# An expert stage in fp32: quarter-row gathers turned on VectorE in place of TensorE, and the gated product's transposes in two groups

## The chip, the core and the metric
The kernel runs on one core of a Trainium2 chip, as one program. The metric is device time in microseconds of one execution. The runs of the kernel before lie within 0.3% of each other. All data are float32.

## What is computed
The reference is one layer of a language model over 2048 prompt tokens and 128 sample tokens: a mixer (depthwise convolution and spatial gating), attention into 256 memory tokens, and a mixture of experts with a final norm. Only the last part matters here:

```python
# hier_moe: top-1 of 4 groups, then top-2 of 8 experts in it; D = 1024, 32 experts of width 512
def expert_block(args):                      # one block of rows that go to one expert
    xb, e = args
    return (jax.nn.silu(xb @ w_eg[e]) * (xb @ w_eu[e])) @ w_ed[e]
...
x = x + hier_moe(rms_norm(x, g_ffn), ...)    # gate weight times each expert's row, added to x
y = rms_norm(x, g_final)
```

## The kernel before, in words
**Stages.** The mixer and attention into memory come first. The last stage (one block of code from line 1289 on) has two parts: 17 tiles of 128 tokens go through scores, values, the router and the placing of each token's two assignments into a table in DRAM; then the expert steps run. The two parts overlap a little: the first expert tile is fetched while the last tiles are still in attention.

**An expert step** (`work(t)` on every engine, tiles t = 0 to 41) takes 64 rows of an expert of the lower 16 and 64 rows of one of the upper 16. The rows are those of `h3_d`, the normalised tokens. TensorE's helper `both` (lines 2206 and 2207) issues two matmuls of 64 stationary columns each, one per expert, into the upper and lower half of a PSUM tile; each is two records in the trace, since the data are fp32. In a step TensorE does, in this order:
- the gate product (8 k-chunks, 512 columns, into `psg`), then the up product in two halves of 256 columns (8 k-chunks each, into `ups[0]`, a part of `r_pss`, and `ups[1]`, a part of `r_psk`);
- `turn_h(t, 0)`: two 128x128 transposes of the first half of the gated product `hb`; `turn_x(t + 1)`: eight transposes of the next tile's gathered rows `xg` into `pst`; `turn_h(t, 1)`: the other two of `hb`;
- the down product (4 k-chunks, two halves of 512 columns, into `psx`), 16 pairs of matmul records.

**VectorE** in a step: `tokens(t + 2)` (one cast of 128 row numbers, line 1957), `rows(t)` (lines 1985 and 1986), `hidden(t)` (two products of silu and up, line 1974), `hT_out` (line 1979), `xT_out(t + 1)` (line 1962, chunks 4 to 7), `add_x(t)` (line 1993: the weighted result added to x, two halves), `scale(t)` (the final norm). **ScalarE**: silu (1770), `hT_out` (1775, the first two chunks in one copy), `xT_out` (1780, chunks 0 to 3), the squares of the final norm (1800). **GpSimd** issues the small transfers: `gather_x(t)` (1608, rows of x), `gather(t + 2)` (1600, rows of h3, 4 KB each), `fetch(t + 3)` and `fetch_again(t + 1)` (1584, two transfers of 64 table rows each), `scatter_x(t)` (1614), a power (1621), `scatter_out(t)` (1627). `gather_x(t)` waits until the scatter of t - 1 has landed.

**SyncE** loads the weights with `load_part` (line 1286), 2 MB each for gate, up and down of an expert, as soon as the slot's last reader of that part is done. The upper experts have one slot, the lower ones two that alternate.

**Order of the work.** Each engine's program is written out by hand, with one counting semaphore per kind of event (`T["h_done"]`, `T["xT_done"]`, ...). `need(eng, sem, n)` is a wait that is left out where n is 0 or less. An engine runs its own program in order, so whatever stands behind a wait waits too.

**The start of the expert steps** has a chain without overlap: the last rank gives the last table scatter, then `fetch(1)`, `tokens(1)` on VectorE, `gather(1)` on GpSimd, `turn_x(1)` on TensorE, the two `xT_out` copies, and the gate product of tile 1. VectorE's program there is `tokens(1)`, `add_x(0)`, a copy of the load list, `tokens(2)`, `xT_out(1)`; GpSimd's is `fetch(1)`, `gather(1)`, `fetch(2)`, `fetch_again(1)`, `scatter_x(0)`.

`turn_split` (line 220) already exists, for the attention tiles. It transposes 32x32 blocks on VectorE, of a tile whose DMA has put the quarter-rows of 32 tokens into each group of 32 partitions. It gives chunk k of the contraction the columns j of which j mod 8 is k.

## Time and profile before
| what | value |
|---|---|
| median of 3 runs | 2452.66 us (2451.31 to 2457.74) |
| the profiled execution: its own time | 2455.3 us |
| its span, first to last instruction | 2453.6 us |
| TensorE busy | 2385.9 us, 97% |
| VectorE busy | 1015.2 us, 41% |
| GpSimd busy | 560.1 us, 23% |
| ScalarE busy | 448.8 us, 18% |
| DMA | 427.31 MB, 174 GB/s over the span |

The span is 1.7 us shorter than the execution's own time, and that execution was 2.6 us above the median. A busy TensorE is one that has a matmul in flight; back-to-back matmuls overlap, so the distance from start to start, not the duration, says what one costs. The expert steps run from 1524.9 us to the end.

### The profile page before, as it was taken

Reading aid. Unit: us, or ns where it says so; the run is one execution under the profiler, and the core shown is the slowest. Engines: PE = TensorE matmul, PEld = TensorE weight load, DVE = VectorE, ACT = ScalarE, POOL = GpSimd, SP = SyncE. Lnnn points to the kernel's source line nnn. Section 1 sums busy time; section 2 is a strip of 40 time slices with the busy share of each in tenths; the row PEclk is TensorE's granted clock in tenths of the full one; section 3 lists DMA queues with packets and bytes.
Section 4 is the critical chain, followed back from the end, with each engine's and each line's share of the span. In section 5 each row is a group of like instructions: output and inputs, shape, how many; then the busy total and the mean of one; then the engine's idle time right before and its main releaser. Section 6 shows DMA issues by size and latency. Waiting matters only on the chain.

```text
span 2453.6 us, 33018 instructions
## 1 busy us (share of the span) xinstructions
PE 2385.9 (97%) x10639; PEld 1161.2 (47%) x10640; DVE 1015.2 (41%) x2549; ACT 448.8 (18%) x1012; POOL 560.1 (23%) x711
## 2 busy tenths in 40 slices
PE   8999999999999997999999998999999999999998
PEld 4444444444444474444444443444444444444443
DVE  1585665666678112255555543222222222222222
ACT  2222212212211122111111111111111111111111
POOL 1122232132133000011111113232323322323231
PEclk9999999999999999999999999999999999999999
DMA  6202111111132436464444327967497749797994
GB/s 238 108 30 67 39 41 58 39 53 47 40 126 106 149 127 223 148 191 124 122 130 127 117 86 271 340 220 270 169 366 264 261 165 368 262 353 270 350 353 149
DMA packets 186898, 427.31 MB, mean 174 GB/s; under 512 B 27874, under 2 KB 51962, under 8 KB 186666
## 3 DMA queue, kind: packets, MB, share of 16 engines
q1 hardware_dynamic: 155810, 351.41, 42.0%
q0 software_dynamic: 30656, 74.14, 8.3%
q8 instruction: 53, 0.87, 0.1%
q10 hardware_dynamic: 336, 0.54, 0.1%
q14 instruction: 43, 0.35, 0.0%
HBM read 351.89 MB, written 88.52 MB: 179 GB/s over the span
## 4 chain that ended last, share of the span: by engine, by line
PE 57%; DMA 1%; DVE 1%; issue 0%; POOL 0%; ACT 0%; POOLq 0%; SPq 0%; DVEq 0%; ACTq 0%
PE r_pss L2206 17%; PE r_psx L2206 12%; PE r_psx L2165 10%; PE r_pss L2145 9%; PE r_psk L2206 6%; PE r_pst L2195 2%; PE r_psr L2177 1%; PE r_psr L2215 1%; PE r_pss L2215 0%; PE r_pss L2207 0%; DMA table_scratch<-r_val,r_slot 0%; PE r_pss L2251 0%; DMA r_x1n<-h_scratch,e_token 0%; PE r_psx L2207 0%; PE r_psk L2207 0%
## 5 line engine op out<-in xcount | busy, mean ns | idle before, releaser
L790 PE MATMUL a_psz<-W 128*128 128x512 f32 x1088 | 480.0, 594 | 0.1
L2206 PE MATMUL r_pss<-W,r_h2T 128*64 x1312 | 432.3, 488 | 3.3 <-issue 3.3
L2207 PE MATMUL r_pss<-W,r_h2T 128*64 128x256 f32 (+1 forms) x1312 | 432.3, 488 | 0.0
L628 DVE SCALAR_TENSOR_TENSOR yacc<-aext,pcol,yacc 128x256 f32<-128x256 f32 x928 | 370.8, 477 | 0.0
L790 PEld LDWEIGHTS a_psz<-W 128*128 128x128 f32 x1088 | 203.2, 191 | 235.5 <-issue 235.0
L2206 PEld LDWEIGHTS r_pss<-W,r_h2T 128*64 128x64 f32 x1312 | 180.1, 137 | 257.3 <-issue 215.8
L2207 PE MATMUL r_psx<-W,r_x1r 128*64 128x512 f32 x656 | 290.3, 595 | 0.0
L2206 PE MATMUL r_psx<-W,r_x1r 128*64 x656 | 290.3, 595 | 0.0
L2165 PE MATMUL r_psx<-W 128*128 128x512 f32 x544 | 237.6, 594 | 1.2 <-ACT W L1724 1.2
L2145 PE MATMUL r_pss<-W,r_h2T 128*128 128x512 f32 x512 | 225.4, 598 | 2.3 <-PEq L123 2.3
L2207 PEld LDWEIGHTS r_pss<-W,r_h2T 128*64 128x64 f32 x1312 | 180.1, 137 | 0.0
L492 POOL TENSOR_TENSOR W<-W 128x512 f32<-128x512 f32 x34 | 115.6, 3408 | 267.0 <-ACT W L605 267.0
L2206 PEld LDWEIGHTS r_psx<-W,r_x1r 128*64 128x64 f32 x656 | 86.5, 137 | 170.7 <-issue 170.7
L2165 PEld LDWEIGHTS r_psx<-W 128*128 128x128 f32 x544 | 102.1, 190 | 123.8 <-issue 123.8
L2145 PEld LDWEIGHTS r_pss<-W,r_h2T 128*128 128x128 f32 x512 | 96.6, 191 | 118.4 <-issue 118.4
L1993 DVE SCALAR_TENSOR_TENSOR r_x<-r_psx,e_spair,r_x 128x512 f32<-128x512 f32 x84 | 63.0, 751 | 213.6 <-PE r_psx L2207 213.6
L2207 PE MATMUL r_psk<-W,r_h2T 128*64 128x256 f32 x656 | 148.3, 379 | 0.0
L2206 PE MATMUL r_psk<-W,r_h2T 128*64 x656 | 148.3, 379 | 0.0
L957 PE MATMUL a_psz<-W,a_maT 128*128 128x512 f32 x272 | 122.3, 592 | 0.0
L957 PE MATMUL a_psz<-W 128*128 128x512 f32 x272 | 122.3, 592 | 0.0
L1614 POOL DMA_INDIRECT x_scratch<-r_x,e_stoken x41 | 42.7, 1042 | 324.7 <-DVE r_x L1993 304.8
L1974 DVE TENSOR_TENSOR r_x1r<-r_pss,r_x1r 128x256 f32<-128x256 f32 x43 | 18.1, 423 | 229.5 <-PE r_pss L2207 229.5
(358 smaller groups left out, 2618.8 us busy)
## 6 DMA issues: line engine op xcount, KB each, us to landing
W<-in_w_expert_gate SPq DMA_DIRECT2D x32, 2048.0 KB, 12.1
W<-in_w_expert_up SPq DMA_DIRECT2D x32, 2048.0 KB, 11.0
W<-in_w_expert_down SPq DMA_DIRECT2D x32, 2048.0 KB, 10.3
W<-in_x_prompt SPq DMA_DIRECT2D x32, 512.0 KB, 4.2
x_scratch<-W SPq DMA_DIRECT2D x18, 512.0 KB, 3.0
r_x1r<-x_scratch SPq DMA_DIRECT2D x17, 512.0 KB, 4.4
x_scratch<-r_x SPq DMA_DIRECT2D x17, 512.0 KB, 5.2
h_scratch<-r_h SPq DMA_DIRECT2D x17, 512.0 KB, 2.6
```

Source lines behind the costliest of these rows:

```text
L492: pool.tensor_tensor(x, mixed[:, 512 * n:512 * n + 512], x, ALU.add).then_inc(S["x1_half"], 1)
L628: ins = dve.scalar_tensor_tensor(out=out, in0=src, scalar=w, in1=yacc[:, i, :], op0=ALU.mult, op1=ALU.add)
L790: last = pe.matmul(psz[bank][:], hT[t.par][:, k, :], w_in[bank][:, k, :], start=(k == 0), stop=(k == KD - 1))
L957: last = pe.matmul(psz[n][:], (maT[:, k, :] if k < CG else mbl[t.par][:, k - CG, :]), w_out[:, k, 512 * n:512 * n + 512], start=(k == 0), ...
L1614: pool.indirect_dma_start(out=x2_d.rearrange("t p d -> (t p) d"), out_offset=bass.IndirectOffsetOnAxis(ap=stoken[t.par][:], axis=0), in_=y ...
L1993: dve.scalar_tensor_tensor(out=yb[t.par][:, c], in0=psx[:, c], scalar=spair[t.par][:, 1:2], in1=yb[t.par][:, c], op0=ALU.mult, op1=ALU.add ...
L2145: last = pe.matmul(pss[:, 2 * n:2 * n + 2, :].rearrange("p h n -> p (h n)"), h2T[i % 2][:, k, :], A[:, k, 512 * n:512 * n + 512], start=(k ...
L2165: last = pe.matmul(psx[:, 512 * n:512 * n + 512], (pT if i else qT)[:, c, :], (B if i else w_xo)[:, c, 512 * n:512 * n + 512], start=(c == ...
L2177: last = pe.matmul(psr[:, 0:NG + NE], h3T[:, k, :], wr[:, k, :], start=(k == 0), stop=(k == KD - 1))
L2195: last = pe.transpose(pst[:, k, :], xg[t.par][:, P * k:P * k + P], ident[:])
L2206: pe.matmul(out[0:HALF, :], xt[:, 0:HALF], W[:, bass.ds(base + at, n)], start=start, stop=stop)
L2207: return pe.matmul(out[HALF:P, :], xt[:, HALF:P], W[:, at:at + n], start=start, stop=stop)
```

## The change
The x rows are gathered as quarter-rows and turned on VectorE:
- `token` gets four columns. `tokens(t)` makes 16 small VectorE operations of 32 partitions each, out of one quarter of the row numbers into another quarter of the partitions, 4 times the number plus the quarter.
- `gather(t)` issues four indirect transfers of 128 quarter-rows (1 KB each) in place of one of 128 rows.
- `turn_x` and the semaphore `x_turned` go; both `xT_out` copies (ScalarE and VectorE) become one `turn_split` on VectorE, which waits for the gathers themselves. `xT_done` counts once a tile.
- `load_part` reads gate and up weights as `a (p k) n` in place of `a (k p) n`, so that the contraction is cut the same way; each partition then reads 8 adjoining rows.

The transposes of the gated product stand elsewhere: `turn_h(t, 0)` between chunks 3 and 4 of the second up half, `turn_h(t, 1)` after the first two of the down product's eight calls of `both`. The down product takes chunk 0, chunk 1, then chunks 2 and 3; ScalarE copies chunks 0 and 1 one by one.

```diff
-                          I[name][0][bass.ds(e, 1), :, :].rearrange("a (k p) n -> p (a k) n", p=P)).then_inc(here, 16)
+                          I[name][0][bass.ds(e, 1), :, :].rearrange("a (k p) n -> p (a k) n" if n == 2 else "a (p k) n -> p (a k) n", p=P)).then_inc(here, 16)
...
-            token = [sb(f"e_token{i}", [P, 1], I32) for i in range(2)]
+            token = [sb(f"e_token{i}", [P, QUADS], I32) for i in range(2)]
...
                     def gather(t):
                         pool.wait_ge(T["token_done"], t.v + 1)
-                        need(pool, T["x_turned"], 2 * (t.v - 1))
+                        need(pool, T["xT_done"], t.v - 1)
                         settle(pool)
-                        pool.indirect_dma_start(out=xg[t.par][:], out_offset=None,
-                                                in_=h3_d[0:P * (EARLY + 2), :] if isinstance(t.v, int) and t.v == 0 else h3_d,
-                                                in_offset=bass.IndirectOffsetOnAxis(ap=token[t.par][:], axis=0)).then_inc(x_here[t.par], 16)
+                        h3_rows = h3_d[0:P * (EARLY + 2), :] if isinstance(t.v, int) and t.v == 0 else h3_d
+                        for b in range(QUADS):
+                            c = D // QUADS
+                            pool.indirect_dma_start(out=xg[t.par][:, c * b:c * b + c], out_offset=None,
+                                                    in_=h3_rows.rearrange("t (q c) -> (t q) c", q=QUADS),
+                                                    in_offset=bass.IndirectOffsetOnAxis(ap=token[t.par][:, b:b + 1], axis=0)).then_inc(x_here[t.par], 16)
...
-                        act.activation(hT[:, 0:2, :], psh[:, 0:2, :], ACT.Copy).then_inc(T["hT_lo"], 1)
-
-                    def xT_out(t):
-                        act.wait_ge(T["x_turned"], 2 * t.v + 1)
-                        need(act, T["up_done"], t.v)
-                        act.activation(xT[t.par][:, 0:4, :], pst[:, 0:4, :], ACT.Copy).then_inc(T["xT_done"], 1)
+                        for k in range(2):
+                            act.activation(hT[:, k, :], psh[:, k, :], ACT.Copy).then_inc(T["hT_lo"], 1)
...
                     def tokens(t):
                         dve.wait_ge(pair_here[t.par], 32 * (t.half + 1))
-                        need(dve, x_here[t.par], 16 * t.half)
-                        dve.tensor_copy(token[t.par][:], pair[t.par][:, 0:1]).then_inc(T["token_done"], 1)
+                        need(dve, x_here[t.par], 16 * QUADS * t.half)
+                        for b in range(QUADS):
+                            for q in range(QUADS):
+                                last = dve.tensor_scalar(token[t.par][QUAD * q:QUAD * q + QUAD, b:b + 1], pair[t.par][QUAD * b:QUAD * b + QUAD, 0:1],
+                                                         float(QUADS), float(q), ALU.mult, ALU.add)
+                        last.then_inc(T["token_done"], 1)
 
                     def xT_out(t):
-                        dve.wait_ge(T["x_turned"], 2 * t.v + 2)
+                        dve.wait_ge(x_here[t.par], 16 * QUADS * (t.half + 1))
                         need(dve, T["up_done"], t.v)
-                        dve.tensor_copy(xT[t.par][:, 4:8, :], pst[:, 4:8, :]).then_inc(T["xT_done"], 1)
+                        turn_split(dve, xT[t.par][:], xg[t.par][:]).then_inc(T["xT_done"], 1)
...
-                        pe.wait_ge(T["xT_done"], 2 * t.v + 2)
+                        pe.wait_ge(T["xT_done"], t.v + 1)
...
                             for k in range(KD):
+                                if m and k == KD // 2:
+                                    turn_h(t, 0)
                                 last = both(ups[m], xT[t.par][:, k, :], base, 4096 + 512 * k + 256 * m, k == 0, k == KD - 1, 256)
                             last.then_inc(T["up_done" if m else "up_half"], 1)
-                        turn_h(t, 0)
-                        if j < LAST - 1:
-                            turn_x(t.at(1), (0, 1, 2, 3))
-                            turn_x(t.at(1), (4, 5, 6, 7))
-                        turn_h(t, 1)
                         pe.wait_ge(down_here, wanted)
                         need(pe, F["added"], 2 * t.v)
-                        for m in range(2):
-                            pe.wait_ge(T["hT_hi" if m else "hT_lo"], t.v + 1)
+                        for k in range(2):
+                            pe.wait_ge(T["hT_lo"], 2 * t.v + k + 1)
                             for n in range(2):
-                                for k in (2 * m, 2 * m + 1):
-                                    last = both(psx[:, 512 * n:512 * n + 512], hT[:, k, :], base, 8192 + 1024 * k + 512 * n, k == 0, k == KE - 1)
-                                if m:
-                                    last.then_inc(T["down_done" if n else "y_half"], 1)
+                                both(psx[:, 512 * n:512 * n + 512], hT[:, k, :], base, 8192 + 1024 * k + 512 * n, k == 0, False)
+                            if k == 0:
+                                turn_h(t, 1)
+                        pe.wait_ge(T["hT_hi"], t.v + 1)
+                        for n in range(2):
+                            for k in (2, 3):
+                                last = both(psx[:, 512 * n:512 * n + 512], hT[:, k, :], base, 8192 + 1024 * k + 512 * n, False, k == KE - 1)
+                            last.then_inc(T["down_done" if n else "y_half"], 1)
```

The same edits are made for tiles 0 and 1, whose code stands outside the steps: `turn_x(0)` between the two halves of the last attention tile's scores goes, `xT_early` on VectorE becomes one `turn_split`, `turn_x(1)` ahead of the steps goes, and `gate_early` waits for `xT_done`.

## Rows read from the trace of the kernel before

**Rows 1.** The page: the chain that ended last, by line, in shares of the span.
```profile
PE r_pss L2206 17%; PE r_psx L2206 12%; PE r_psx L2165 10%; PE r_pss L2145 9%; PE r_psk L2206 6%; PE r_pst L2195 2%; PE r_psr L2177 1%; PE r_psr L2215 1%; PE r_pss L2215 0%; PE r_pss L2207 0%; DMA table_scratch<-r_val,r_slot 0%; PE r_pss L2251 0%; DMA r_x1n<-h_scratch,e_token 0%; PE r_psx L2207 0%; PE r_psk L2207 0%
```

**Rows 2.** Groups by line and shape from 1400 us on: busy us, mean ns | idle before, releaser.
```profile
L2195 PE MATMUL r_pst<-ident,r_x1n 128*128 128x128 f32 x336 | 44.5, 276 | 7.1 <-DMA r_x1n<-h_scratch,e_token 7.1
```

**Rows 3.** TensorE's timeline around one step's transposes: start us, us, engine, line, operation.
```profile
2007.96 0.38 PE L2206 MATMUL r_psk<-W,r_h2T 128*64 x1
...
2008.17 0.38 PE L2206 MATMUL r_psk<-W,r_h2T 128*64 x1
...
2008.49 0.44 PE L2215 MATMUL r_psr<-ident,r_x1r 128*128 128x128 f32 x2
...
2009.95 0.64 PE L2206 MATMUL r_psx<-W,r_x1r 128*64 x1
...
2010.43 0.59 PE L2206 MATMUL r_psx<-W,r_x1r 128*64 x1
...
2030.74 0.44 PE L2215 MATMUL r_psr<-ident,r_x1r 128*128 128x128 f32 x2
```

**Rows 4.** TensorE's timeline around the first tile's x transposes, in the attention stage.
```profile
1441.52 1.04 PE L2195 MATMUL r_pst<-ident,r_x1n 128*128 128x128 f32 x8
1442.39 1.45 PE L2145 MATMUL r_pss<-W,r_h2T 128*128 128x512 f32 x3
```

**Rows 5.** VectorE's timeline in one step.
```profile
1999.38 0.14 DVE L1985 CAST e_stoken<-e_spair 128x1 int32<-128x1 f32 x1
1999.44 0.14 DVE L1986 CAST f_oidx<-e_spair 128x1 int32<-128x1 f32 x1
2005.22 0.42 DVE L1974 TENSOR_TENSOR r_x1r<-r_pss,r_x1r 128x256 f32<-128x256 f32 x1 [5.63 <-PE r_pss L2207]
2008.61 0.43 DVE L1974 TENSOR_TENSOR r_x1r<-r_psk,r_x1r 128x256 f32<-128x256 f32 x1 [2.96 <-PE r_psk L2207]
```

**Rows 6.** VectorE's timeline early in the kernel: line 663 in a loop over partition halves.
```profile
27.42 1.14 DVE L663 TENSOR_SCALAR W<-W 64x576 f32<-64x576 int32 x2
```

**Rows 7.** Timelines of VectorE, GpSimd and TensorE where the expert stage starts; one granted clock.
```profile
1446.95 2.03 DVE L222 STREAM_TRANSPOSE r_h3T<-r_h3s 128x1024 f32<-128x1024 f32 x1 [4.92 <-DMA r_h3s<-h_scratch]
...
1515.82 0.15 DVE L1957 CAST e_token<-e_pair 128x1 int32<-128x1 f32 x1 [6.62 <-DMA e_pair<-table_scratch]
...
1517.14 1.03 POOL L1600 DMA_INDIRECT r_x1n<-h_scratch,e_token  x1 [5.14 <-issue]
...
1519.40 0.52 POOL L1584 DMA_DIRECT2D e_pair<-table_scratch  x1 [0.63 <-issue]
...
1522.48 0.15 DVE L1957 CAST e_token<-e_pair 128x1 int32<-128x1 f32 x1 [5.01 <-DMA e_pair<-table_scratch]
...
1524.90 1.11 PE L2206 MATMUL r_pss<-W,r_h2T 128*64 x1 [0.98 <-issue]
...
1519.60:1529.70 10.10, 6.77 (x20) 3.06 (x22) 2.62 (x7) 1.93 (x5) 5.11 (x9) 0.50 0.43 148
```

**Rows 8.** GpSimd's timeline in one step.
```profile
2018.67 1.04 POOL L1614 DMA_INDIRECT x_scratch<-r_x,e_stoken  x1 [10.13 <-DVE r_x L1993]
...
2028.78 1.00 POOL L1608 DMA_INDIRECT r_x<-x_scratch,e_stoken  x1 [5.10 <-DMA x_scratch<-r_x,e_stoken]
2030.08 0.96 POOL L1600 DMA_INDIRECT r_x1n<-h_scratch,e_token  x1 [0.30 <-issue]
...
2034.48 0.52 POOL L1584 DMA_DIRECT2D e_spair<-table_scratch  x1 [0.73 <-issue]
```

**Rows 9.** Issue to landing of line 1600 (x gathers), then of line 1584 (pair fetches).
```profile
DMA to landing us min/median/max: 4.4/7.7/10.2
...
DMA to landing us min/median/max: 1.7/5.5/8.6
```

**Rows 10.** Busy time by stretch: PE, PEld, DVE, ACT, POOL, clock, DMA share, GB/s.
```profile
2000.00:2100.00 100.00, 100.00 (x650) 48.24 (x648) 22.01 (x48) 13.60 (x31) 31.49 (x41) 1.00 0.98 353
...
5.00:10.00 5.00, 1.89 (x9) 1.75 (x9) 0.73 (x3) 2.16 (x3) 3.68 (x7) 1.00 1.05 394
```

More of the change, by code:

```diff
@@ L1409, in build @@
             e_names = ("counted listed turned placed sorted link steps_known slots_known loads_known count_known "
-                     "token_done stoken_done x_turned xT_done gate_done up_half up_done down_done y_half silu_done h_done h_turned "
+                     "token_done stoken_done xT_done gate_done up_half up_done down_done y_half silu_done h_done h_turned "
                      "hT_lo hT_hi").split()
@@ L1687, in work @@
                             for i in range(2):
-                                pool.wait_ge(x_here[i], 16 * (pairs + LAST // 2))
+                                pool.wait_ge(x_here[i], 16 * QUADS * (pairs + LAST // 2))
                                 settle(pool)
@@ L1787, in _ @@
                     for m in range(2):
-                        act.activation(hT[:, 2 * m:2 * m + 2, :], psh[:, 2 * m:2 * m + 2, :], ACT.Copy).then_inc(T["hT_hi" if m else "hT_lo"], 1)
-                    act.wait_ge(S["s_psum"], NT - 1)
-                    xT_out(fixed(1))
+                        act.activation(hT[:, 2 * m:2 * m + 2, :], psh[:, 2 * m:2 * m + 2, :], ACT.Copy).then_inc(T["hT_hi" if m else "hT_lo"], 1 if m else 2)
                     def squares(t):
@@ L1808, in work @@
                         hT_out(t)
-                        if j < LAST - 1:
-                            xT_out(t.at(1))
-                        else:
-                            act.wait_ge(T["xT_done"], 4 * (pairs + 2))
-                            settle(act)
+                        if j == LAST - 1:
                             act.wait_ge(F["sample_here"], 16)
@@ L2014, in xT_early @@
                         dve.wait_ge(S["s_psum"], NT - 2)
-                        dve.wait_ge(T["x_turned"], 2)
-                        for m in range(2):
-                            dve.tensor_copy(xT[0][:, 4 * m:4 * m + 4, :], pst[:, 4 * m:4 * m + 4, :]).then_inc(T["xT_done"], 1)
+                        dve.wait_ge(x_here[0], 16 * QUADS)
+                        turn_split(dve, xT[0][:], xg[0][:]).then_inc(T["xT_done"], 1)
                     for s in range(NT):
@@ L2134, in turn_p @@
                         pe.wait_ge(S["prob_done"], i)
-                        pe.wait_ge(T["xT_done"], 2)
+                        pe.wait_ge(S["squares1"], NT - 1)
                         for k in range(KD):
@@ L2189, in ranks @@
                         pe.matmul(psk[:, 0:NE], ones[:], total[:], start=False, stop=True).then_inc(S["rank_psum"], 1)
-                    def turn_x(t, ks):
-                        if ks[0] == 0:
-                            pe.wait_ge(x_here[t.par], 16 * (t.half + 1))
-                            need(pe, T["xT_done"], 2 * t.v)
-                        for k in ks:
-                            last = pe.transpose(pst[:, k, :], xg[t.par][:, P * k:P * k + P], ident[:])
-                        if ks[-1] in (3, 7):
-                            last.then_inc(T["x_turned"], 1)
                     def weights(t):
@@ L2211, in turn_h @@
                         if m == 0:
-                            need(pe, T["hT_lo"], t.v)
+                            need(pe, T["hT_lo"], 2 * t.v)
                             need(pe, T["hT_hi"], t.v)
@@ L2231, in work @@
                             for k in range(KD):
+                                if m and k == KD // 2:
+                                    turn_h(t, 0)
                                 last = both(ups[m], xT[t.par][:, k, :], base, 4096 + 512 * k + 256 * m, k == 0, k == KD - 1, 256)
                             last.then_inc(T["up_done" if m else "up_half"], 1)
-                        turn_h(t, 0)
-                        if j < LAST - 1:
-                            turn_x(t.at(1), (0, 1, 2, 3))
-                            turn_x(t.at(1), (4, 5, 6, 7))
-                        turn_h(t, 1)
                         pe.wait_ge(down_here, wanted)
                         need(pe, F["added"], 2 * t.v)
-                        for m in range(2):
-                            pe.wait_ge(T["hT_hi" if m else "hT_lo"], t.v + 1)
+                        for k in range(2):
+                            pe.wait_ge(T["hT_lo"], 2 * t.v + k + 1)
                             for n in range(2):
-                                for k in (2 * m, 2 * m + 1):
-                                    last = both(psx[:, 512 * n:512 * n + 512], hT[:, k, :], base, 8192 + 1024 * k + 512 * n, k == 0, k == KE - 1)
-                                if m:
-                                    last.then_inc(T["down_done" if n else "y_half"], 1)
+                                both(psx[:, 512 * n:512 * n + 512], hT[:, k, :], base, 8192 + 1024 * k + 512 * n, k == 0, False)
[6 more added lines that the diff above has]
+                            last.then_inc(T["down_done" if n else "y_half"], 1)
                     def product(out, k, at, stop):
@@ L2257, in gate_early @@
                             pe.wait_ge(S["exp_done"], NT - 1)
+                            pe.wait_ge(T["xT_done"], 1)
                         for k in ks:
```

6 lines of the change are left out of this document (removed).

## The prediction, made before the changed kernel was run

> **What bounds the kernel now.** I read the chain that ended last first, since it says which engine's work the end hangs on. Of the expert stage it holds the gate, up and down products, and also 2% of `r_pst L2195`, the transposes of the gathered rows: about 49 us that multiply nothing [rows 1]. Next, TensorE's waits: over all 336 of these transposes (42 tiles of 8) it stood still before them for 7.1 us in total, and that in one place, the stage's start [rows 2]. So in the steps TensorE waits for nobody, and a step lasts as long as TensorE takes to issue it. Two steps' transposes stand at 2008.49 and 2030.74, which makes 22.25 us a step [rows 3]. An instruction taken off TensorE shows in the time at once; one given to another engine is free as long as that engine keeps up. The start of the stage is the other way round: there TensorE waits for a chain through VectorE, GpSimd and a DMA.
>
> **TensorE's part of a step.** Pairs of 256-column matmuls start 0.215 us apart (2007.96, 2008.17), so 512 columns take 0.43. From the last up pair at 2008.17 to the second down pair at 2010.43 are 2.26 us; less 0.215 and 0.43, the twelve transposes between cost 1.615 [rows 3]. A transpose by itself: eight from 1441.52 to 1442.39, 0.109 each, 12 make 1.31 [rows 4]. The other 0.31 is what it costs to go into the group and out of it: the first transpose comes 0.32 after the last pair, not 0.215, and the second down pair 0.48 after the first, not 0.43.
>
> After the change four transposes are left, 4 x 0.109 = 0.44, in two groups. What a group costs beyond its own time no row shows for the new places. Bounds: 0.31, as the group behind 256-column pairs has it [rows 3], and nothing, as the group between 512-column matmuls of the attention stage, from which the next matmul starts right behind the eighth transpose [rows 4]. The group in the second up half is of the first kind, and I take 0.31; the one in the down product stands between 512-column pairs, but of 64 stationary columns, and the wait for the down weights stays behind the up pairs, so I take half, 0.15. New: 0.44 + 0.31 + 0.15 = 0.90, a saving of 0.72 a step (0.56 with both at 0.31, 1.18 with both at nothing). Forty steps turn a next tile (42 less tiles 0 and 1): 40 x 0.72 = **28.7 us**, bounds 22.4 and 47. The last step has no x to turn, but it has the two groups; from its own gap I put 0.3. Tile 0's eight transposes leave the attention stage, where TensorE is busy on both sides: 0.87 [rows 4].
>
> **Do the moved transposes find their data?** `turn_h(t, 0)` needs the first gated half, a product of 0.42 us from 2005.22 on, done at 2005.64 [rows 5]. The second up half's first pair is 15 x 0.215 before 2008.17, at 2004.95; eight pairs later is 2006.67: 1.0 us to spare. The second half's product starts at 2008.61 and ends at 2009.04 [rows 5]; the new `turn_h(t, 1)` comes four down pairs after the up half's end, at 2008.39 + 1.72 = 2010.1: 1.1 to spare. Its copy (0.42 to 0.43 like the products) has the 1.72 us of chunk 1 as cover. If one of them came late, TensorE would stand for the difference.
>
> **VectorE's part.** `tokens` goes from one operation to 16. Bounds for one: 0.06, as the casts at 1999.38 and 1999.44 follow each other [rows 5], and 0.18. The upper one comes from a loop that, like the new one, changes the group of partitions from one operation to the next with no wait between: two of 0.55 us take 1.14 together, so the second starts only when the first has ended, 0.03 later [rows 6]; with 0.15 for a small operation [rows 7] that is 0.18. I take 0.18, the row of the same kind: 15 x 0.18 = 2.7 more. In a step VectorE idles 5.63 us before the first gated half [rows 5], so 2.7 fit, and 2.9 are left. The 32x32 transpose of a tile takes 2.03 [rows 7]; in a step it stands after the second copy, about 1.94 + 0.6 into the down product, and ends at 4.6, before three quarters of that product (5.15), where `add_x` can begin. Cost nothing; if VectorE were late there, `scale` and the next `hidden` would be.
>
> The Trainium skill ("VectorE: DVE Perf Modes", section "Two Vector instructions with no wait between them") has this as a rule: an instruction whose output starts in another quadrant than the last one's is held until all earlier ones have finished. By that rule each of the 16 is held; the trace agrees. Were it not so, the start below would be 3.6 us cheaper.
>
> **GpSimd's part.** Three more gathers; one follows another after 1.3 us (2028.78 to 2030.08) [rows 8]: 3.9 us a step. It idles 10.13 us before this scatter, 5.10 before this `gather_x` [rows 8], so they are covered unless the loop under the slower rival closes. The 0.5 MB a tile stay the same.
>
> **The start of the stage**, where nothing covers. Before: `tokens(1)` at 1515.82, gather at 1517.14, second transfer of `fetch(2)` at 1519.40, `tokens(2)` at 1522.48, gate product at 1524.90 [rows 7]. After: the gathers begin 2.7 later, at 1519.84, and the fourth at 1523.74; the fetch, 2.26 behind the last gather as before, at 1526.0; it lands as before 3.08 later, 1529.1. `tokens(2)` stands before `xT_out(1)` on VectorE, so the transpose waits for it: 1529.1 + 16 x 0.18 + 2.03 = 1534.0, and the gate product starts at 1534.2: **9.3 us later** (5.6 with operations of 0.06). The rows themselves have landed by then (4.4 to 10.2 after the issue [rows 9]; above 8.2 they would be last). TensorE's clock stands at 0.50 from 1519.6 to 1529.7 [rows 7], half speed, after it had been idle; it will again fall in the longer idle time and rise after a stretch of work. Before, 5 us of gate product ran at half speed; I put no difference, within 1 us either way.
>
> **The rest at nothing:** ScalarE loses a copy and gets one more; the one transpose for tile 0 on VectorE takes some 0.8 us more than two copies, ahead of a softmax whose result TensorE takes up much later; the weights' new order moves the same bytes in longer runs.
>
> **Sum:** -28.7 - 0.3 - 0.9 + 9.3 = -20.6. Against the profiled execution, 2455.3 (its span and 1.7 around it), that is 2434.7; that execution was 2.6 above the median of 2452.66, so I predict **2432 us**, 0.84% less. Its own range: at best 0.87 a step (one group at 0.31, one at nothing), 5.6 for the start and 1 us of the clock, 2421; at worst 0.56 a step and 10.3, 2440.
>
> **Rivals.**
> 1. *Both groups cost nothing beyond themselves.* 40 x 1.18 = 47 saved, in all -39: 2414. For it: the attention stage's group [rows 4]. Against: the group behind 256-column pairs cost 0.31 [rows 3]. Chance 0.07.
> 2. *The DMA engines become the bound of the steps with loads.* From 2000 to 2100 their share is 0.98 at 353 GB/s [rows 10]; a step shorter by 0.72 with the same bytes asks for 365. If these steps (27 loads of 6 MB lie in 40 steps) keep 22.25 us, only 13 x 0.72 = 9.4 are saved, in all about -2: **2451**. Against: 394 GB/s have been moved at 5 to 10 us [rows 10], and longer runs should not be slower. Chance 0.11.
> 3. *GpSimd's queue becomes the loop: slower.* A scatter at 2018.67 must land before `gather_x` at 2028.78, the last fetch starts at 2034.48 [rows 8]; 3.9 more puts it at 2038.4, and a landing of 8.6 [rows 9] at 2047.0. VectorE needs the pairs before it can make the next gated half, at 2005.22 + 2 x 22.25 - 0.7 = 2049.0, and TensorE has 1.0 behind that: 3.0 us of slack. The gathers' landings show 7.7 as median and 4.4 as least [rows 9], so other traffic costs them 3.3. If that price goes by the number of descriptors, four times as many could make it 13, 10 more. It decides from 3.8 us of added latency on: 0.8 x 25 loaded steps = 20, the saving. At 4.5 more: 1.5 x 25 = 38, in all +17: **2470**. Against: the bytes are the same, and most waits of the queue have slack. Chance 0.12. 
> 4. *The change doesn't do what it says*: a moved group waits for its data and takes the saving back. The margins of 1.0 and 1.1 us speak against it; a loss of 0.3 a step gives 2444. Chance 0.05.
>
> **The numbers.** The forecast has 0.65. Within 0.3% (7.4 us, about what a measurement of this kernel can tell from no change) lies rival 2, and slower is rival 3. Faster: 0.65 + 0.07 + 0.05 = 0.77. The range 2421 to 2451 takes in the forecast's own and rivals 2 and 4, and leaves out 0.07 and 0.12.
>
> **What the profile will show.** No L2195; two groups of two transposes per step, the distance between steps 21.5 us; sixteen operations of VectorE 0.18 apart; four gathers 1.3 apart; the first gate product of the steps near 1533. I am wrong if steps lie more than 21.8 us apart with TensorE not waiting (a group costs more), if TensorE waits for `hb` copies or weights in loaded steps (rivals 4 and 2), if VectorE waits for `e_spair` (rival 3), or if the start is over 11 us later.

## The result, and the profile after

The changed kernel measured **2484.3 us** (median of 4, 2483.1 to 2486.9) beside 2452.0 for the one before: 1.0128 times as long, interval 1.011 to 1.0146. The forecast was 2432, so by this measurement it was wrong, on the other side. It is also a number that did not come back: the same kernel, unedited, in five later measurements on four chips, took 2440.8, 2437.6, 2437.8, 2440.4 and 2440.9, that is 0.9928 to 0.9946 times the kernel before (intervals within 0.9907 to 0.9967). The kernel before took 2451.0 to 2457.7 beside the 2484 and 2450.5 to 2456.3 beside the five, so whatever made 2484 left it alone. (One execution of the kernel before, beside the first edits, took 5140 us; it stands alone, is in no ratio, and nothing shows its cause.) Both have to be read: what made 2484, and what the change is worth without it.

First the profile of the 2484 execution (span 2481.4). Its page, the chain that ended last, by engine:

```profile
PE 48%; another core or an unknown queue 7%; issue 2%; DVE 1%; DMA 1%; POOL 0%; ACT 0%; POOLq 0%; SPq 0%; ACTq 0%; DVEq 0%
```

Seven per cent hang on something that the profile can't name. The chain of waits by engine, from 1534 to 2440 (who waited for whom: us, times, longest), for TensorE, then ScalarE and VectorE:

```profile
PE r_psx L2192 <- ACT r_x1r L1779: 17.0, 12, 1.7
PE r_psx L2192 <- DVE r_x1r L1975: 13.3, 19, 1.2
...
ACT r_x1r L1779 <- remote: 99.0, 13, 7.8
...
DVE r_x1r L1975 <- remote: 62.0, 19, 3.9
```

TensorE waits for the two copies of the turned gated product (L1779 on ScalarE, L1975 on VectorE), and these wait for something that the profile calls "remote", which is an update that it can match to no instruction's end, though all that they need is TensorE's own transposes. The two rows add up to 30.3 us, where the prediction had nothing. The timeline of one such step:

```profile
1654.06 0.44 PE L2201 MATMUL r_psr<-ident,r_x1r 128*128 128x128 f32 x2
1654.07 0.95 POOL L1603 DMA_INDIRECT r_x1n<-h_scratch,e_token  x1 [0.30 <-issue]
...
1655.33 0.94 POOL L1603 DMA_INDIRECT r_x1n<-h_scratch,e_token  x1 [0.30 <-issue]
...
1656.00 0.38 PE L2193 MATMUL r_psk<-W,r_h2T 128*64 128x256 f32 x1
1656.27 1.18 POOL L1584 DMA_DIRECT2D e_pair<-table_scratch  x2
1657.37 1.10 POOL L1584 DMA_DIRECT2D e_spair<-table_scratch  x2
1657.48 0.45 ACT L1779 ACTIVATE r_x1r<-r_psr 128x128 f32<-128x128 f32 x2 [7.80 <-remote]
1657.56 0.42 DVE L1970 TENSOR_TENSOR r_x1r<-r_psk,r_x1r 128x256 f32<-128x256 f32 x1 [4.61 <-PE r_psk L2193]
...
1658.00 0.64 PE L2192 MATMUL r_psx<-W,r_x1r 128*64 x1 [1.62 <-ACT r_x1r L1779]
```

The two transposes end at 1654.50 and the last up product at 1656.38. Both tell the other engines by a semaphore (`h_turned` and `up_done`), and both signals arrive close together, at 1657.4 and 1657.5: 2.9 and 1.2 us late. TensorE itself went on without a gap until it needed the copy. I call these *late updates*. Counted from the trace's semaphore events, 35 of the 81 recorded updates of `h_turned`, 27 of the 41 of `up_done` and 3 of the 41 of `up_half` came over 0.3 us after their instruction's end (the expectations below say 36 of 78 for `h_turned`: a first count over a shorter stretch, in which an update without a record passed for a late one). No recorded update of ScalarE or VectorE did, though that trace misses 19 of the 82 of `h_done`; in the trace of before none of any engine's was late. Every one of them overlaps a stretch in which GpSimd issues gathers or fetches.

Now the same kernel in after_fourth (span 2437.5). Its chain by line, which answers to [rows 1], holds no transposes of rows any more, and 2% for the gated product's:

```profile
PE r_pss L2192 16%; PE r_psx L2192 11%; PE r_psx L2160 10%; PE r_pss L2140 9%; PE r_psk L2192 6%; PE r_psr L2172 1%; PE r_psr L2201 1%; PE r_pss L2201 1%; PE r_pss L2238 0%; DMA x_scratch<-r_x,e_stoken 0%; PE r_pss L2193 0%; PE r_psx L2276 0%; PE r_psx L2193 0%; PE r_psk L2193 0%; PE r_psk L2184 0%
```

TensorE's waits over the stretch from 1534 to 2440:

```profile
PE r_pss L2192 <- issue: 2.5, 1, 2.5
PE r_psr L2201 <- DVE r_x1r L1970: 1.2, 1, 1.2
```

and the rows of one of its steps on TensorE, which answer to [rows 3]:

```profile
2041.64 0.38 PE L2192 MATMUL r_psk<-W,r_h2T 128*64 x1
...
2041.96 0.44 PE L2201 MATMUL r_psr<-ident,r_x1r 128*128 128x128 f32 x2
2042.33 0.43 PE L2192 MATMUL r_psk<-W,r_h2T 128*64 x1
...
2042.60 0.38 PE L2192 MATMUL r_psk<-W,r_h2T 128*64 x1
...
2043.89 0.38 PE L2192 MATMUL r_psk<-W,r_h2T 128*64 x1
...
2044.11 0.59 PE L2192 MATMUL r_psx<-W,r_x1r 128*64 x1
...
2045.39 0.59 PE L2192 MATMUL r_psx<-W,r_x1r 128*64 x1
...
2045.92 0.44 PE L2201 MATMUL r_pss<-ident,r_x1r 128*128 128x128 f32 x2
2046.29 0.64 PE L2192 MATMUL r_psx<-W,r_x1r 128*64 x1
...
2046.77 0.59 PE L2192 MATMUL r_psx<-W,r_x1r 128*64 x1
...
2063.64 0.44 PE L2201 MATMUL r_psr<-ident,r_x1r 128*128 128x128 f32 x2
```

From one step's first group to the next: 2063.64 - 2041.96 = 21.68, where before had 22.25. In the 2484 execution the shortest distance is 21.68 too, and most lie at 22.4 to 23.6, 22.93 on average, against 21.82 in after_fourth: (22.93 - 21.82) x 40 = 44 us, and the two spans differ by 43.9.

Where the 16.1 us between before's and after_fourth's profiled spans come from (each segment is a difference of two starts in the timelines; the routing stage's last product is that of `p_at_place`):

| segment | before | after_fourth | difference |
|---|---|---|---|
| start to the routing stage's last product | 1514.66 | 1514.51 | -0.15 |
| from there to the first gate product of the steps | 10.24 | 14.15 | +3.9 |
| to the first group of `r_psr` transposes | 16.32 | 14.71 | -1.6 |
| 40 distances from step to step | 892.58 | 872.70 | -19.9 |
| to the end | 19.83 | 21.45 | +1.6 |

The third and the last go together: the group now stands 1.7 earlier in its step. The first segment alone is between 1511.3 and 1517.3 in the profiled executions of this study, so the spans can't be compared closer than some 3 us without such a ledger. The second is not the change's cost alone either: 2.3 of it hang on when one fetch landed in the profile of before (see the start, below).

### The profile page after: what moved, and what is told of

It is laid out like the page before. It is cut to its first block, busy times and chain, and to the rows that moved or that the text cites. A ratio compares the mean times of both kernels' runs of the same rounds, so it can differ in the third digit from the quotient of the medians.

```text
span 2481.4 us, 33004 instructions
## 1 busy us (share of the span) xinstructions
PE 2370.8 (96%) x10303; PEld 1120.8 (45%) x10304; DVE 1166.0 (47%) x3178; ACT 427.4 (17%) x1012; POOL 682.8 (28%) x837
## 3 DMA queue, kind: packets, MB, share of 16 engines
q0 software_dynamic: 32672, 74.15, 8.2%
## 4 chain that ended last, share of the span: by engine, by line
PE 48%; another core or an unknown queue 7%; issue 2%; DVE 1%; DMA 1%; POOL 0%; ACT 0%; POOLq 0%; SPq 0%; ACTq 0%; DVEq 0%
PE r_pss L2192 14%; PE r_psx L2160 9%; PE r_psx L2192 9%; PE r_pss L2140 8%; PE r_psk L2192 4%; PE r_psr L2172 1%; PE r_psk L2193 0%; PE r_pss L2238 0%; PE r_pss L2201 0%; PE r_psr L2201 0%; PE r_pss L2193 0%; DMA x_scratch<-r_x,e_stoken 0%; DVE r_x1r L1975 0%; PE r_psx L2276 0%
## 5 line engine op out<-in xcount | busy, mean ns | idle before, releaser
L2192 PE MATMUL r_psx<-W,r_x1r 128*64 x656 | 301.7, 598 | 32.1 <-ACT r_x1r L1779 17.0
L2193 PE MATMUL r_psx<-W,r_x1r 128*64 128x512 f32 x656 | 301.9, 598 | 0.0
L1603 POOL DMA_INDIRECT r_x1n<-h_scratch,e_token x168 | 161.6, 962 | 66.8 <-issue 60.0
L2192 PE MATMUL r_psk<-W,r_h2T 128*64 x656 | 157.1, 382 | 0.0
L2193 PE MATMUL r_psk<-W,r_h2T 128*64 128x256 f32 x656 | 157.1, 382 | 0.0
L222 DVE STREAM_TRANSPOSE r_h2T<-r_x1n 128x1024 f32<-128x1024 f32 x58 | 117.7, 2030 | 5.6 <-DMA r_gffn<-in_g_ffn 5.5
L1796 ACT ACTIVATE r_x1r<-r_x 128x512 f32<-128x512 f32 x84 | 53.0, 631 | 383.3 <-DVE r_x L1989 382.9
```

The source lines that it names most:

```text
L222: return dve.transpose(dst.rearrange("p k (b r) -> p b k r", r=QUAD), src.rearrange("p (b a k) -> p b k a", b=QUADS, a=QUAD))
L1603: pool.indirect_dma_start(out=xg[t.par][:, c * b:c * b + c], out_offset=None, in_=h3_rows.rearrange("t (q c) -> (t q) c", q=QUADS), in_off ...
L1796: act.activation(junk_f, yb[t.par][:, 512 * m:512 * m + 512], ACT.Square, scale=1 / 32, accum_out=fss[:, t.par, m:m + 1]).then_inc(F["squa ...
L2192: pe.matmul(out[0:HALF, :], xt[:, 0:HALF], W[:, bass.ds(base + at, n)], start=start, stop=stop)
L2193: return pe.matmul(out[HALF:P, :], xt[:, HALF:P], W[:, at:at + n], start=start, stop=stop)
```

## The experiments

Theory 1 was that GpSimd's gathers cause the late updates; theory 2 blamed the new places, theory 3 the weights' order.

**One gather.** Leaves out the quarter-row order of the rows; the 16 small operations are kept and write plain row numbers (shortened):

```diff
-for b in range(QUADS): pool.indirect_dma_start(out=xg[...][:, c * b:c * b + c], ... token[...][:, b:b + 1] ...)
+pool.indirect_dma_start(out=xg[t.par][:], in_=h3_rows, ... token[t.par][:, 0:1] ...)
```

> Edit of the changed kernel: one gather of whole rows in place of four of quarter rows; the same bytes, a quarter of the row pieces, and the 16 small operations that make the indices are kept. The rows arrive in an order that the products don't expect, so the numbers it computes are not the reference's. In the changed kernel 36 of the 78 updates of the semaphore h_turned and most of up_done reach ScalarE or VectorE 0.2 to 2.9 us after TensorE's last transpose or product has ended, always while GpSimd has its gathers and fetches one behind another. THEORY 1 (GpSimd's row of four gathers holds TensorE's updates back): no late updates any more, steps 21.7 us apart, some 45 us of waiting gone, and 3.8 us less at the start: 2484 - 49 = about 2437. THEORY 2 (the new places of the transposes are to blame, gathers have no part): 2480 or more, only the start is shorter. THEORY 3 (the slower steps come from the DMA traffic of the weights in their new order): 2480 or more.

Measured: **2433.5**, ratio 0.9916 (0.9899 to 0.9932); 39 distances of 21.68 to 21.73 and one of 24.39 where the loop ends; no late update. As theory 1 had it, but the runs below, which keep four gathers and have no late update either, show that this proved nothing.

**Four gathers of 32 rows.** Each fills its own 32 partitions with whole rows.

> Edit of the changed kernel: four gathers, but each of 32 whole rows into its own 32 partitions, so the number of instructions is that of the changed kernel and the number of row pieces (128 in all, not 512) and the bytes are those of one gather. Its contraction order is not the reference's. If THEORY 1 holds and what counts is the number of instructions in a row, it stays at 2484 within 8; if what counts is the number of row pieces (GpSimd's writing of them), the late updates go and it comes near 2440. By THEORIES 2 and 3 it stays at 2480 or more, as one_gather does too.

Measured: 2446.0, ratio 0.9969 (0.9958 to 0.9979); no late update. Four distances stand out (23.3 to 26.6), one of them the loop's end, which all versions have; in the profile it is above all TensorE waiting 5.2 us for the first gated half. Why this form is 12 us slower than one gather stays open.

**The transposes back behind the up product, the four quarter-row gathers kept.**

```diff
-                                if m and k == KD // 2:
-                                    turn_h(t, 0)
...
+                        turn_h(t, 0)
+                        turn_h(t, 1)
                         pe.wait_ge(down_here, wanted)
...
-                            if k == 0:
-                                turn_h(t, 1)
```

> Edit of the changed kernel: the four transposes of the gated product go back behind the up product, two and two, nothing else. THEORY 1: the updates still come late while GpSimd gathers, now with no product between the transposes and the down product that needs them; a step without late updates is some 22.1 us (the second gated half, 0.43, and its copy are waited for), and with them on top the time is 2490 to 2530, above the changed kernel. THEORY 2: no late updates, steps of 22.1, 40 x 0.4 above the 2439 that the changed kernel would have without waits: about 2455, below the changed kernel. THEORY 3: as the changed kernel plus 0.4 a step, 2500.

Measured: **2441.0**, ratio 0.9952 (0.9936 to 0.9969). Once more, beside after_third:

> The changed kernel with its four transposes of the gated product behind the up product, again, in the same call as after_third. By THEORY 4a, if after_third is at 2484, this one is late as well, at 2490 or more, unless the late updates need the new places (THEORY 1b), in which case it stays at 2441 within 4. If after_third is near 2440 it repeats 2441.

Measured: 2443.7, ratio 0.9963 (0.9943 to 0.9982). The timeline of old_places:

```profile
1846.73 0.97 POOL L1603 DMA_INDIRECT r_x1n<-h_scratch,e_token  x1 [0.30 <-issue]
...
1847.60 0.44 PE L2201 MATMUL r_psr<-ident,r_x1r 128*128 128x128 f32 x2
1847.71 0.42 DVE L1970 TENSOR_TENSOR r_x1r<-r_psk,r_x1r 128x256 f32<-128x256 f32 x1 [2.96 <-PE r_psk L2193]
1848.01 0.95 POOL L1603 DMA_INDIRECT r_x1n<-h_scratch,e_token  x1 [0.30 <-issue]
1848.08 0.45 ACT L1779 ACTIVATE r_x1r<-r_psr 128x128 f32<-128x128 f32 x2 [6.59 <-PE r_psr L2201]
...
1848.19 0.44 PE L2201 MATMUL r_pss<-ident,r_x1r 128*128 128x128 f32 x2 [0.15 <-DVE r_x1r L1970]
1848.67 0.42 DVE L1975 COPY r_x1r<-r_pss 128x256 f32<-128x256 f32 x1 [0.53 <-PE r_pss L2201]
```

The gathers lie right over the transposes, and each copy starts 0.04 after them. So a row of four gathers is not enough to make updates late. Theory 1 as it stood, by which this was to be 2490 to 2530, falls. And the step is 21.79 to 21.90, hardly longer than with the new places; theories 1 and 2 had 22.1.

**The gathers moved** behind `rstd(t)`.

> Edit of the changed kernel: GpSimd's four gathers of tile t+2 move from behind gather_x(t) to behind rstd(t), in the loop's steps only, so that they run while TensorE is in the next tile's gate product, where its only update is gate_done, and that one has some time to spare. THEORY 1: h_turned and up_done come in time, steps 21.7 to 21.9 apart: 2435 to 2450, faster than both kernels. If gate_done now comes late by 2 us and the first gated half with it, some of it stays: up to 2465. THEORIES 2 and 3: 2480 to 2487.

Measured: 2451.8, ratio 0.9998 (0.9985 to 1.001). No late update, yet slower than the unedited kernel's 2438 to 2441 and just above the 2450 of theory 1: in its waits VectorE stands for the rows that `add_x` needs and for the gathered rows, and TensorE for both.

```profile
PE r_pss L2192 <- DVE r_h2T L222: 7.3, 3, 3.6
PE r_psr L2201 <- DVE r_x1r L1970: 5.0, 6, 1.2
...
DVE r_x L1989 <- DMA r_x<-x_scratch,e_stoken: 99.1, 22, 7.7
...
DVE r_h2T L222 <- DMA r_x1n<-h_scratch,e_token: 36.6, 17, 6.3
```

The gathers now begin 13.8 us behind a step's first group of transposes (median), where they began 1.1 behind it in after_fourth, and the rows land too late in some steps. Their old place was the better one. No update was late, as in all the runs after the first measurement.

**The kernel itself again.** After these the suspect was the first measurement.

> The changed kernel itself, unedited, once more and on the chip of this call. With the four transposes back in their old places and the four gathers kept (old_places), no update of TensorE's was late, although the gathers lay over them in the same way, and the time was 2441: gathers alone don't make the updates late. THEORY 1b (the late updates need both: the new places and the four quarter-row gathers): 2484 within 4 again, with 30 or more late updates in its profile. THEORY 4 (the late updates are a matter of the execution or the chip and not of the program): no late updates, steps 21.7 apart, about 2438 to 2441.

Measured: 2440.8, ratio 0.994 (0.9924 to 0.9957), no late update. A third and a fourth time:

> The changed kernel, unedited, a third time, in a call of its own. It measured 2484 at first, with late updates, and 2441 in after_again, with none. THEORY 4a (the late updates belong to one chip, or to one placement of the program): either 2484 within 4 with 30 or more late updates, or 2436 to 2442 with none, and nothing between. THEORY 4b (they come and go from execution to execution): times between the two, and some late updates in any profile.

> The changed kernel, unedited, a fourth time, beside the three edits of this call. THEORY 4a: 2436 to 2442 with no late update, or 2484 within 4 with 30 or more of them; then the other three tell what else is slow on that chip.

Measured: 2437.6 (0.9907 to 0.9952) and 2437.8 (0.9911 to 0.9944), none late. Twice more:

> The changed kernel, unedited, a fifth time, on whatever chip this call gets. Four chips so far: the first one (2484, 36 of 78 h_turned updates late) and three others (2438 to 2441, none late). THEORY 4a: 2484 within 4 if it is the first chip or the first placement again, otherwise 2436 to 2442.

> The changed kernel, unedited, once more, beside turn_before_tokens_again. THEORY 4a: 2436 to 2442 and no late update, or 2484 within 4 and 30 or more late ones.

Measured: 2440.4 (0.9922 to 0.9967) and 2440.9 (0.9926 to 0.9965), none late. Theory 4b, times between the two, falls: of the 21 executions of this program the first four took 2483 to 2487 and the other 17 took 2436 to 2442. The two values are what theory 4a foresaw; that they belong to a chip or to a placement, as it also says, is not shown.

**The kernel before with four gathers.**

> Edit of the kernel before: its one gather of whole rows a tile becomes four of quarter rows (four small operations of VectorE make their indices); TensorE's transposes of rows and gated product stay as they are. THEORY 1 (GpSimd's row of four gathers is enough): TensorE's updates late in most steps, 2480 or more. THEORY 1b and 4: none late; the start is some 3 us longer, and the rest hidden: 2454 to 2458.

Measured: 2456.3, ratio 1.0007 (0.9998 to 1.0017); steps 22.25, none late. Three more gathers a tile are hidden.

**The weights' order alone, in the kernel before.** Rows and weights don't match in it.

> Edit of the kernel before: only the gate and up weights come in the changed kernel's order (each partition's rows side by side), with the gathered rows as they were, so that the sums are over mismatched pairs and the output isn't the reference's. My theory: the same bytes in longer runs move nothing that TensorE waits for: 2453 within 3, steps 22.25. THEORY 3 (the longer runs change the DMA engines' traffic, for better or worse): over 5 us either way.

Measured: 2452.2, ratio 0.9994 (0.9985 to 1.0004), steps 22.25, none late. The longer runs change nothing that TensorE waits for in this kernel; theory 3 falls.

**The new places alone, in the kernel before** (shortened; the down product takes its chunks in the changed kernel's order, while ScalarE still copies chunks 0 and 1 in one):

```diff
+                                if m and k == KD // 2:
+                                    turn_h(t, 0)
...
-                        turn_h(t, 0)
                         if j < LAST - 1: turn_x(t.at(1), ...)
-                        turn_h(t, 1)
...
+                            if k == 0:
+                                turn_h(t, 1)
```

> Edit of the kernel before: only the gated product's transposes move to the changed kernel's places, two in the second up half and two after the first down products; the rows' eight transposes stay on TensorE behind the up product. If each group costs its own time and some 0.3 (0.53 for the one in the up product and 0.47 for the one in the down product, as in after_again), the step has 0.53 + 0.47 + 8 x 0.109 + 0.3 = 2.2 in place of 1.6: 22.25 + 0.57 = 22.8 us a step, 41 x 0.57 = 23 more in all, 2476. RIVAL: splitting costs nothing, since the wait for copies that it removes is worth as much: 2453 within 4. If late updates come from the places alone, they show here as well, and the time is over 2485.

Measured: **2481.3**, ratio 1.0109 (1.0092 to 1.0126), none late. TensorE in one step:

```profile
2042.13 0.44 PE L2215 MATMUL r_psr<-ident,r_x1r 128*128 128x128 f32 x2
...
2044.38 1.09 PE L2195 MATMUL r_pst<-ident,r_x1n 128*128 128x128 f32 x8
2045.40 0.64 PE L2206 MATMUL r_psx<-W,r_x1r 128*64 x1
...
2047.27 0.44 PE L2215 MATMUL r_pss<-ident,r_x1r 128*128 128x128 f32 x2
2047.63 0.64 PE L2206 MATMUL r_psx<-W,r_x1r 128*64 x1
```

The step is 22.85, 0.60 more (0.57 expected); the loop's end took 27.11 in place of 24.79, with the granted clock at 0.50 for 3.4 us. TensorE waits for no copy in this profile. The same twelve transposes cost more in three groups than in one: each further group costs some 0.3. On a TensorE that waits for nobody, the new places lose.

**Tile 1 turned before tile 2's indices are made**, two lines of VectorE's queue exchanged:

```diff
-                    tokens(fixed(2))
                     dve.wait_ge(S["s_psum"], NT - 1)
                     xT_out(fixed(1))
+                    tokens(fixed(2))
```

> Edit of the changed kernel: at the stage's start VectorE turns tile 1's rows before it makes tile 2's indices, not after. In after_again the indices of tile 2 took VectorE from 1525.5 to 1528.0 and the transpose 1528.0 to 1530.1, and the gate product began 0.2 later. If the start is bound by VectorE's order (my theory), the transpose begins when the last quarter has landed, at most 3.3 us after the fourth gather's issue at 1522.2, and the gate product begins some 2.5 us sooner after the routing stage's last product: 11.7 in place of 14.2, and about 2 us come off the time. RIVAL: the rows land only near 1528, and nothing is gained; or the later gather of tile 2 stops TensorE in the next step, and nothing is left.

> The changed kernel with tile 1's rows turned before tile 2's indices are made, a second time, on another call's chip: 2435 within 3, about 3 below after_sixth if that one is near 2438. Should after_sixth stand at 2484, this kernel has the same four gathers and the same places and should have late updates too, at about 2480.

Measured: **2435.4**, ratio 0.9922 (0.9905 to 0.9938), after_fourth beside it 2437.8; again **2433.1**, ratio 0.9913 (0.9896 to 0.9929), beside 2440.9. The fastest version of this study that leaves nothing out. The second pair lies 7.8 apart where 3 were expected; of the 6.9 between its two profiled spans, 3.5 lie at the start that the edit touches, and the rest in stretches that it doesn't (2.2 ahead of it, 1.2 in the steps). The start in both, first after_fourth, then this one:

```profile
1513.38 2.52 DVE L1951 TENSOR_SCALAR e_token<-e_pair 32x1 int32<-32x1 f32 x16 [4.34 <-DMA e_pair<-table_scratch]
...
1516.74 1.03 POOL L1603 DMA_INDIRECT r_x1n<-h_scratch,e_token  x1 [4.58 <-DVE e_token L1951]
...
1520.60 0.95 POOL L1603 DMA_INDIRECT r_x1n<-h_scratch,e_token  x1 [0.30 <-issue]
1521.56 1.13 POOL L1584 DMA_DIRECT2D e_pair<-table_scratch  x2
...
1523.91 2.52 DVE L1951 TENSOR_SCALAR e_token<-e_pair 32x1 int32<-32x1 f32 x16 [6.41 <-DMA e_pair<-table_scratch]
...
1526.46 2.01 DVE L222 STREAM_TRANSPOSE r_h2T<-r_x1n 128x1024 f32<-128x1024 f32 x1
...
1528.66 1.11 PE L2192 MATMUL r_pss<-W,r_h2T 128*64 x1 [13.97 <-issue]
```

```profile
1518.33 0.95 POOL L1603 DMA_INDIRECT r_x1n<-h_scratch,e_token  x1 [0.30 <-issue]
...
1521.10 2.01 DVE L222 STREAM_TRANSPOSE r_h2T<-r_x1n 128x1024 f32<-128x1024 f32 x1 [5.88 <-issue]
...
1523.31 1.11 PE L2192 MATMUL r_pss<-W,r_h2T 128*64 x1 [11.56 <-issue]
```

From the fourth gather to the gate product 4.98 in place of 8.06, and 11.75 in place of 14.15 after the routing stage's last product: 2.4 sooner, against 2.5 expected. In the second pair the last distance is 11.04 in place of 14.59.

## Why the prediction was wrong, and where it was right

**The recorded number: wrong.** No term of the sum accounts for the 52 us between 2432 and 2484. Of the rivals, number 4 has the right place (a moved group's copy is late), but gave it 0.3 a step and the data as its cause. What failed is the step "Do the moved transposes find their data?", in what it assumed and didn't write: that a copy starts when the transposes before it have ended. In that execution it started up to 2.9 later, and TensorE waited 30.3 us for the two copies, which were put at nothing; the whole difference from after_fourth is 44. The margins themselves hold: in the profiles of the five repeats TensorE never waits for a copy. Why TensorE's updates were late there **stays open**. Shown is what is not enough: four gathers (old_places, before_four_gathers), the new places (before_h_places), both together (five repeats). But no edit was measured where the unedited kernel was slow, so whether the late updates also need one of these is not known; they all overlap GpSimd's issuing. The chip, the placement of the program in memory, or other work on that chip are left, and no run tells them apart; the record does not name the first measurement's chip.

**The change's own worth**, with no late updates: 2437.6 to 2440.9, in the range of 2421 to 2451 and 6 to 9 above the forecast of 2432; 0.54 to 0.72% faster. That it comes so near is in part luck: by the table above the distances from step to step saved 8.8 less than forecast, and the start cost 5.4 less. The 0.9 for tile 0's transposes and the 0.3 for the last step are too small for any row here to show.

- *TensorE's part of a step: right mechanism, mis-sized.* Forecast 0.72 a step, measured 22.25 - 21.68 = 0.57. The group in the up product costs what was put down: from the pair before it to the next one (2041.64 to 2042.33) 0.69, less the 0.215 of a pair, then 0.05 more in the next interval, 0.53 in all against 0.22 + 0.31. The group in the down product costs 2046.29 - 2045.39 - 0.43 = 0.47 and 0.05 more in the next interval, 0.52 against 0.22 + 0.15: the full 0.3 here too, so halving it between the two bounds was the error. 1.615 - 0.53 - 0.52 = 0.57: the lower bound was the right value. Over the 38 distances without an exception this saves 21.7; the forecast had 28.7 over 40.
- *Not in the forecast: two steps that gave some back.* Where the loop ends the distance is 26.02 in place of 24.79. TensorE idles there 2.48 us, 2.32 before; in after_fourth the granted clock then stands at 0.50 for 3.4 us, and the gate products behind the gap last 1.11 as at the stage's start. Before shows no such stretch there, and one_gather and turn_before_tokens, without it, have 24.4. It comes and goes in the same program: after_fifth idles 2.50 us, stays at 1.00 and has 24.40, so the stretch costs some 1.6. Before, before_four_gathers and before_weights_order lack it too, at 2.3 to 2.4 of idle time; whether the change makes it more frequent is not shown. And at `pool.drain()` ahead of the last scatter but one GpSimd waits 13.0, before 11.5, VectorE's `scale` behind it holds up the next `hidden`, and TensorE waits 1.2 (1.0 to 2.3 in the five repeats).
- *The start: right in kind, too dear.* Forecast 9.3 later, measured 3.9. `tokens` takes 2.52 for 16, where I had put 2.9: 0.8 for the two. From the fourth gather's issue to `tokens(2)` are 3.3 (1520.60 to 1523.91), where I had put 2.26 + 3.08 from the kernel before: 2.0. These two are errors of the forecast. Another 2.3 of the 5.4 missed are not: `tokens(1)` starts 1.1 ahead of the routing stage's last product, where it had been 1.2 behind it, since its pairs landed sooner. From the landing of the last table scatter to `tokens(1)` are 7.2 us in the profile of before, but 5.4 to 6.0 in three edits of that kernel and 4.9 to 5.6 in the six profiles of the changed kernel, so most of this is that one execution's. From `tokens(1)` to the gate product are 15.3 in place of 9.1: 6.2 is the better figure for what the change costs there. The path was named rightly, as turn_before_tokens shows. That VectorE's order made part of the cost, and could be changed, I didn't see.
- *VectorE: each small operation held.* Sixteen in 2.52 are 0.157 each: one of 0.145 starts 0.013 after the last has ended. I took 0.18. That is the rule of the Trainium skill ("VectorE: DVE Perf Modes", section "Two Vector instructions with no wait between them"), and the trace agrees.
- *GpSimd's queue (rival 3): it did not close.* Gathers 1.26 to 1.33 apart as forecast, and TensorE never waits for it in the repeats. The extra price feared for 512 row pieces, 10 us, isn't there: issue to landing of one transfer is, in after_fourth (76 of 156 gathers have a recorded landing) and then in the kernel before,

```profile
DMA to landing us min/median/max: 2.7/6.1/10.0
```

```profile
DMA to landing us min/median/max: 5.1/7.8/10.2
```

  Each of the four carries a quarter of the bytes, though, and they are issued 3.8 us apart in all: a whole tile's rows are there 11.3 us after the first issue (median of 19 tiles) in place of 7.8. So four gathers bring a tile later, by 3.5 and not by 10 or more, and that is hidden in the steps. The software queue's packets rise from 30656 to 32672 (the page), though the gathers' row pieces grew fourfold. The 2016 more are 16 for each of the 3 x 42 added gathers, and the page has them all among the packets under 512 bytes (27874 to 29891), so the rows' own packets are no more than before: four quarter-row pieces share one. The Trainium skill ("DMA: Bandwidth & Descriptors", section "Queues, rings and completion order") says that a packet holds several descriptors; whether its packets are the ones that the profile's page counts, no run here shows.
- *DMA as the bound (rival 2): no.* From 2000 to 2100 the engines moved more in after_fourth, 368 against 353 GB/s [rows 10], and TensorE was busy throughout:

```profile
2000.00:2100.00 100.00, 100.00 (x597) 42.26 (x595) 40.71 (x114) 11.42 (x32) 43.60 (x55) 1.00 0.96 368
```

**Which part earns it.** Taking the rows off TensorE alone, with the gated product's transposes behind the up product, gives 2441.0 and 2443.7, steps of 21.83. The new places add 0.15 a step, 6 us at most, of which the medians show 0 to 6. They pay only where the eight transposes between the two pairs are gone: without these, old_places waits 0.15 for the second gated half (its row at 1848.19). Put into the kernel before, which had no such wait, they cost 26.4 (2481.3 - 2454.9), of which some 2 lie at the loop's end.

## What to carry to other kernels

On an engine that waits for nobody, count groups and not only instructions: each place where transposes break into a stream of products cost 0.3 us beyond their own time, so splitting a group pays only where it removes a longer wait. At a stage's start, look at the order in one engine's queue: what the next engine needs goes ahead of what only the tile after needs. And a surprising measurement should be repeated, on other chips too, before its profile is explained and before edits are compared with it; I read some 60 late updates as GpSimd's doing, because they coincided with it, and the next edits said nothing about them, since by the five repeats the unedited kernel, too, would most likely have had none by then.

## What I had not expected of the hardware

Semaphore updates of one engine can reach the others up to 2.9 us late while that engine goes on working. One measurement of six of the same program had it (its profiled execution; the other three took as long, 2484 to 2487); in the trace it shows as waits for "remote" with long gaps ahead of copies whose producer had ended. And after some 2.5 us without work at the loop's end the granted clock fell to 0.50 for 3.4 us in four of the five repeats and stayed at 1.00 in the fifth, worth some 1.6 us.
